# Delta inverse in tiles of 32 and 64, a small projection in four strips, an earlier first norm and a seventh place for expert weights

## The reference, cut to what matters

```
mod  = silu(cond) @ w_mod + b_mod                    # shift1, scale1, gate1, shift2, scale2, gate2
h    = layer_norm(x) * (1 + scale1) + shift1
proj = h @ w_in                                      # among it beta, alpha, i, f: 32 columns
# gated DeltaNet, per direction, head and chunk of 64 tokens:
strict_l = where(strict, beta * (k k^T) * decay, 0)
sol  = triangular_solve(eye + strict_l, [v * beta | k * beta * exp(G)])
u    = u_v - u_k @ s;  o = q_dec @ s + qk @ u;  s = s * g_end + k_dec^T @ u
x    = layer_norm(alpha * x + gate1 * mix, ln1_g, ln1_b)
h    = layer_norm(x) * (1 + scale2) + shift2
hid  = silu(h @ w_e1[e]) * (h @ w_e3[e])             # 2 experts per token, of 32; D_EXPERT = 256
x    = layer_norm(alpha * x + gate2 * sum(gate * hid @ w_e2[e]), ln2_g, ln2_b)
```

## Time and profile before

| | |
|---|---|
| median of 3 runs | 1314.59 us (1314.35 to 1315.8) |
| profiled execution | 1314.85 us, span 1313.1 us, clock granted 0.983 |
| PE busy | 1220.2 us, 93% (its weight loads 728.8) |
| DVE, ACT, POOL busy | 653.3, 288.8, 127.0 us |
| DMA | 221.97 MB, mean 169 GB/s; HBM read 211.52 MB, written 17.78 MB |

### The profile page before, as it was taken

How to read it: one execution, slowest core, us unless ns; L and a number is a source line. 1 busy time by engine, 2 the same in 40 slices (tenths; PEclk the granted TensorE clock), 3 DMA queues, 4 the chain that set the end, 5 groups by cost and what they waited for, 6 DMA issues and landing times. The chain is left out here.

```text
span 1313.1 us, 15161 instructions
## 1 busy us (share of the span) xinstructions
PE 1220.2 (93%) x5699; PEld 728.8 (56%) x5699; DVE 653.3 (50%) x1425; ACT 288.8 (22%) x591; POOL 127.0 (10%) x148
## 2 busy tenths in 40 slices
PE   3899999999999999999999999999999898899775
PEld 1455555556557678566666666665459533344332
DVE  5140366658825435245556675342777434243226
ACT  2200354336134324321111020111001001011002
POOL 0000000000000000000000424420300222122010
PEclk9999999999999999999999999999998999999888
DMA  9533332444022213032110212417519799999936
GB/s 370 233 106 117 129 128 83 174 145 94 28 63 54 78 23 104 1 105 84 56 63 25 96 49 94 179 58 208 212 48 389 267 411 420 420 420 419 411 148 251
DMA packets 64972, 221.97 MB, mean 169 GB/s; under 512 B 21390, under 2 KB 32286, under 8 KB 48254
## 3 DMA queue, kind: packets, MB, share of 16 engines
q1 hardware_dynamic: 59566, 209.39, 42.5%
q0 software_dynamic: 5184, 10.50, 2.1%
q10 hardware_dynamic: 144, 1.05, 0.2%
HBM read 211.52 MB, written 17.78 MB: 175 GB/s over the span
## 5 line engine op out<-in xcount | busy, mean ns | idle before, releaser
L505 PE MATMUL bank<-hT,ring 128*128 128x512 f32 x320 | 165.3, 598 | 0.0
L2943 PE MATMUL bank<-ew,xgT 128*64 128x512 f32 (+2 forms) x544 | 130.8, 622 | 17.9 <-DMA ew<-in_experts 16.1
L506 PEld LDWEIGHTS bank<-hT,ring 128*128 128x128 f32 x320 | 60.8, 190 | 76.5 <-issue 76.5
L2943 PEld LDWEIGHTS bank<-ew,xgT 128*64 128x64 f32 (+2 forms) x544 | 47.5, 144 | 98.3 <-issue 96.0
L981 PE MATMUL bank<-hT,ring 128*128 128x512 f32 x176 | 90.4, 595 | 3.0 <-DVE yA L1487 3.0
L1782 PE MATMUL bank<-hT,w_ab 128*128 128x512 f32 x160 | 81.9, 594 | 0.0
L2957 PE MATMUL bank<-ew,hidT 128*64 128x512 f32 (+2 forms) x272 | 67.4, 629 | 8.2 <-DMA ew<-in_experts 7.1
L2315 PE MATMUL bank<-w_out,mT 128*128 128x512 f32 x160 | 70.9, 604 | 3.2 <-PEq L1655 3.2
L506 PE MATMUL bank<-hT,ring 128*128 128x128 f32 x320 | 61.5, 274 | 0.0
L982 PEld LDWEIGHTS bank<-hT,ring 128*128 128x128 f32 x176 | 33.4, 190 | 42.1 <-issue 42.1
L3079 DVE SCALAR_TENSOR_TENSOR uh<-uh,bank 128x256 f32<-128x256 f32 x18 | 7.6, 421 | 97.8 <-ACT uh L3028 97.8
(11 more groups left out here) (521 smaller groups left out, 2175.7 us busy)
## 6 DMA issues: line engine op xcount, KB each, us to landing
ew<-in_experts SPq DMA_DIRECT2D x96, 1024.0 KB, 27.4
ring<-in_blocks SPq DMA_DIRECT2D x10, 2048.0 KB, 9.5
mhalf<-in_mods SPq DMA_DIRECT2D x16, 1024.0 KB, 5.1
w_p<-in_merge SPq DMA_DIRECT2D x14, 768.0 KB, 5.8
w_ab<-in_merge SPq DMA_DIRECT2D x10, 768.0 KB, 4.4
mstage<-in_mods SPq DMA_DIRECT2D x3, 2048.0 KB, 18.3
w_out<-in_w_out SPq DMA_DIRECT2D x1, 4096.0 KB, 15.0
rows<-mod_rows SPq DMA_DIRECT2D x8, 512.0 KB, 7.3
```

What stands on the lines that cost most here:

```text
L505: pe.matmul(lat[:, :], w, hT[:, k, P:T], start=(k == 0), stop=(k == KD - 1))
L506: mm = pe.matmul(ctx[:, 0:P], w, hT[:, k, 0:P], start=(k == 0), stop=(k == KD - 1))
L2943: mm = pe.matmul(bank[2 + n % 2][hs, :], xgT[:, n % 2, k, hs], ew1[w][k // 4][:, 512 * (k % 4):512 * (k % 4) + 512], start=(k == 0), stop= ...
```

## The change

Four parts. The first norm: DVE makes 1/std and a shift (-mean/std) of a tile as soon as the statistics of the next one are done, and ACT normalises tiles 0 to 3; DVE keeps the last. The fourth block of `in_mods` is loaded in two halves. The small projection goes round four strips of 32 output partitions, all 512-token products first and the 128-token ones behind; a matrix of four stacked unit matrices of 32 (`spn`, three DVE additions) sums the strips in a real product in place of the transpose. The delta inverse: f5 and x5 are 16 products of 32 rows by 32 columns by 32, one for each (head, direction, chunk), in place of 8 of 128 x 128 x 64; dT is 8 products of 64x64 with the unit matrix in place of 8 transposes of 128x128, and one ACT copy of 256 columns in place of two of 512; f6 and x6 use 64 rows of weights; the copies of f5 and f6 are 128 and 256 columns, not 512. The experts: a seventh place of first weights lies where x1 was; x1 is written to DRAM (`residual_rows`) a tile at a time in "out", and read back after the last expert load.

```
-            for m in MODS:
+            for m in MODS[:3]:
                 sp.dma_start(mod_at[m], A["mods"][m]).then_inc(got_mod[m], 16)
+            for f in range(2):
+                sp.dma_start(mod_at[3][:, 2048 * f:2048 * f + 2048], A["mods"][3][:, 2048 * f:2048 * f + 2048]).then_inc(
+                    got_last if f else got_mod[3], 16)
...
+                if t:
+                    act.wait_ge(vs.sem, vs.after("shift", t - 1))
+                    act.activation(x_sb[:, t - 1, :], x_sb[:, t - 1, :], ACT.Identity, scale=rstd[:, t - 1:t],
+                                   bias=shift[:, t - 1:t]).then_inc(as_.step("xn", t - 1), 1)
...
-            for t in range(NT):
-                dve.wait_ge(as_.sem, as_.after("sqrt", t))
-                dve.reciprocal(rstd[:, t:t + 1], rstd[:, t:t + 1]).then_inc(vs.step("rec", t), 1)
-                dve.wait_ge(vs.sem, vs.after("rec", t))
-                dve.tensor_scalar(x_sb[:, t, :], x_sb[:, t, :], mv[:, t, 0:1], rstd[:, t:t + 1], ALU.subtract,
-                                  ALU.mult).then_inc(vs.step("xn", t), 1)
+                if t:
+                    dve.wait_ge(as_.sem, as_.after("sqrt", t - 1))
+                    dve.reciprocal(rstd[:, t - 1:t], rstd[:, t - 1:t]).then_inc(vs.step("rec", t - 1), 1)
+                    dve.wait_ge(vs.sem, vs.after("rec", t - 1))
+                    dve.scalar_tensor_tensor(shift[:, t - 1:t], mv[:, t - 1, 0:1], -1.0, rstd[:, t - 1:t], ALU.mult,
+                                             ALU.mult).then_inc(vs.step("shift", t - 1), 1)
...
             pe.wait_ge(vs.sem, vs.after("xn", NT - 1))
+            pe.wait_ge(as_.sem, as_.after("xn", NT - 2))
...
-            for k in range(KD):
-                pe.matmul(bank[6][0:32, :], w_small[:, k, :], hT[:, k, P:T], start=(k == 0), stop=(k == KD - 1))
-                mm = pe.matmul(bank[7][0:32, 0:P], w_small[:, k, :], hT[:, k, 0:P], start=(k == 0), stop=(k == KD - 1))
+            for out, cs in ((bank[6][:, :], slice(P, T)), (bank[7][:, 0:P], slice(0, P))):
+                for k in range(KD):
+                    lo = 32 * (k % 4)
+                    mm = pe.matmul(out[lo:lo + 32, :], w_small[:, k, :], hT[:, k, cs], start=(k < 4), stop=(k >= 4))
...
+                        pe.wait_ge(v1.sem, v1.after("fold", 2))
                         for t in range(NT):
-                            mm = pe.transpose(bank[6][:, 32 * t:32 * t + 32], tr[0:32, tok(t)], ident[0:32, 0:32])
+                            mm = pe.matmul(bank[6][:, 32 * t:32 * t + 32], tr[:, tok(t)], spn[:, 0:32], start=True, stop=True)
...
+            for i in range(2):
+                dve.tensor_tensor(spn[:, 32 * i:32 * i + 32], ident[:, 64 * i:64 * i + 32], ident[:, 64 * i + 32:64 * i + 64],
+                                  ALU.add).then_inc(v1.step("fold", i), 1)
+            dve.wait_ge(v1.sem, v1.after("fold", 1))
+            dve.tensor_tensor(spn[:, 0:32], spn[:, 0:32], spn[:, 32:64], ALU.add).then_inc(v1.step("fold", 2), 1)
...
+    STRIPS = [(d, c) for c in range(2) for d in range(2)]
+    strip_of = lambda d, c: slice(64 * c + BS * d, 64 * c + BS * d + BS)
+    half_of = lambda d: slice(64 * d, 64 * d + 64)
+    inside = lambda h, s: slice(P * h + s.start, P * h + s.stop)
...
-                for d in range(2):
-                    for h in range(H):
-                        cols = dt_[g % 2][d][:, P * h:P * h + P].rearrange("p (b c) -> p b c", c=BS)[:, 1 - d::2, :]
-                        mm = pe.matmul(bx[:, 256 * d + 64 * h:256 * d + 64 * h + 64], n_all[:, tile_of(g, d), d, h, :], cols, start=True, stop=True)
+                for h in range(H):
+                    for d, c in STRIPS:
+                        to, of = strip_of(d, c), strip_of(1 - d, c)
+                        mm = pe.matmul(bx[to, BS * h:BS * h + BS], n_all[of, tile_of(g, d), d, h, to], dt_[g % 2][d][of, inside(h, of)],
+                                       start=True, stop=True)
                 mm.then_inc(p3.step("f5", g), 1)
 
             def inner_product(g):
                 pe.wait_ge(a3.sem, a3.after("f5", g))
                 if g:
                     pe.wait_ge(v3.sem, v3.after("qkm", g - 1, 1))
-                for d in range(2):
-                    for h in range(H):
-                        mm = pe.matmul(by[:, 256 * d + 64 * h:256 * d + 64 * h + 64], hd(dd_[d], h), f_[:, d, h, :], start=True, stop=True)
+                for h in range(H):
+                    for d, c in STRIPS:
+                        to = strip_of(d, c)
+                        mm = pe.matmul(by[to, BS * h:BS * h + BS], dd_[d][to, inside(h, to)], f_in[to, BS * h:BS * h + BS],
+                                       start=True, stop=True)
                 mm.then_inc(p3.step("x5", g), 1)
 
             def turned(g):
                 pe.wait_ge(v3.sem, v3.after("x5", g))
-                for d in range(2):
-                    for h in range(H):
-                        mm = pe.transpose(hd((bx, by)[d], h), hd(dt_[g % 2][d], h), ident)
-                    mm.then_inc(p3.step("dT", g, d), 1)
-
-            def outer(g):
-                pe.wait_ge(a3.sem, a3.after("dT", g, 0))
                 for h in range(H):
                     for d in range(2):
-                        half, c = slice(64 * d, 64 * d + 64), P * h + 64 * (1 - d)
-                        mm = pe.matmul(bx[half, 256 * d + 64 * h:256 * d + 64 * h + 64], n_all[:, tile_of(g, d), d, h, half],
-                                       dt_[g % 2][d][:, c:c + 64], start=True, stop=True)
+                        half = half_of(d)
+                        mm = pe.matmul(bx[half, 64 * h:64 * h + 64], dt_[g % 2][d][half, inside(h, half)], ident[half, half],
+                                       start=True, stop=True)
+                mm.then_inc(p3.step("dT", g), 1)
+
+            def outer(g):
+                pe.wait_ge(a3.sem, a3.after("dT", g))
+                for h in range(H):
+                    for d in range(2):
+                        to, of = half_of(d), half_of(1 - d)
+                        mm = pe.matmul(bx[to, 64 * h:64 * h + 64], n_all[of, tile_of(g, d), d, h, to], dt_[g % 2][d][of, inside(h, of)],
+                                       start=True, stop=True)
                 mm.then_inc(p3.step("f6", g), 1)
...
                     for d in range(2):
-                        half, c = slice(64 * d, 64 * d + 64), P * h + 64 * d
-                        mm = pe.matmul(by[half, 256 * d + 64 * h:256 * d + 64 * h + 64], dT_(g, d)[:, c:c + 64], f_[:, d, h, :],
-                                       start=True, stop=True)
+                        half = half_of(d)
+                        mm = pe.matmul(by[half, 64 * h:64 * h + 64], dT_(g)[half, h, :], f_[half, h, :], start=True, stop=True)
                 mm.then_inc(p3.step("x6", g), 1)
...
                 act.wait_ge(p3.sem, p3.after(x, g))
-                act.activation(f_[:].rearrange("p d h c -> p (d h c)"), bx[:, :], ACT.Copy).then_inc(a3.step(x, g), 1)
+                if x == "f5":
+                    act.activation(f_in, bx[:, 0:H * BS], ACT.Copy).then_inc(a3.step(x, g), 1)
+                else:
+                    act.activation(f_[:].rearrange("p h c -> p (h c)"), bx[:, 0:H * 64], ACT.Copy).then_inc(a3.step(x, g), 1)
 
             def turned(g):
-                for d in range(2):
-                    act.wait_ge(p3.sem, p3.after("dT", g, d))
-                    act.activation(dT_(g, d)[:], (bx, by)[d][:, :], ACT.Copy).then_inc(a3.step("dT", g, d), 1)
+                act.wait_ge(p3.sem, p3.after("dT", g))
+                act.activation(dT_(g)[:].rearrange("p h c -> p (h c)"), bx[:, 0:H * 64], ACT.Copy).then_inc(a3.step("dT", g), 1)
...
-        (mT1_off + 24576, mT1_off + 32768), (rows_off + 8192, rows_off + 16384), (rows_off + 24576, rows_off + 32768)))]
+        (mT1_off + 24576, mT1_off + 32768), (rows_off + 8192, rows_off + 16384), (rows_off + 24576, rows_off + 32768),
+        (yA_off, yA_off + 8192)))]
...
+    slot1 = lambda x: x % 7 if x < NE else (x - NE + 4) % 6
+    in_slot = lambda x: [y for y in range(x + 1) if slot1(y) == slot1(x)]
...
                 sp.dma_start(h2d[t * P:t * P + P, :], h2[:, t % 3, :]).then_inc(sent8[t % 3], 16)
+                sp.dma_start(x1d[t * P:t * P + P, :], x1[:, t, :]).then_inc(x1_sent, 16)
...
     def sync_units(sp):
         def first_half(expert, x, i):
-            sp.wait_ge(pt_m.sem[("f1a", "f1")[i]], user_of(x - 6) + 1)
-            load_half(sp, EXPERT(expert), x % 6, i)
+            if x == 6:
+                sp.wait_ge(x1_sent, 16 * NT)
+            else:
+                sp.wait_ge(pt_m.sem[("f1a", "f1")[i]], user_of(in_slot(x)[-2]) + 1)
+            load_half(sp, EXPERT(expert), x, i)
...
-        for i in range(2):
-            for x in (NSTAT, NSTAT + 1):
-                first_half(expert_of(x), x, i)
+        assert NSTAT == 6
+        for x in (NSTAT, NSTAT + 1):
+            first_halves(expert_of(x), x)
...
         rest(NP)
```

(30 more changed lines are left out.)

53 lines of the change are left out of this document (33 added, 20 removed).

## The result

The changed kernel takes 1299.53 us (median of 4 runs, 1298.06 to 1300.74) against 1315.19 (4 runs of before): ratio 0.988, interval 0.986 to 0.990. 1299.3 was forecast. The profiled execution has a span of 1297.3 us, 15.8 less than before.

| place | start before | lead of the changed kernel |
|---|---|---|
| first block product (L505, now L528) | 53.96 | 6.05 |
| behind the fold of the small projection | 63.23 | 5.44 |
| end of the delta stage (L1183) | 525.85 | 17.06 |
| merge, ahead of the normalisation of `h_f` (L1892) | 741.33 | 17.16 |
| merge, behind it (L1892) | 779.09 | 12.08 |

The account below looks back on a forecast made before the run. TensorE was taken to bound the kernel up to 1029 us, then the expert-weight loads. Terms 0 - 5.6 - 7.2 - 2.7 = -15.5 took 1314.85 to 1299.3 us (chance 58%), range 1292.5 to 1307.5.

Parts of the forecast that it names:

- the two regimes: Whole kernel: TensorE bounds from 60 to 1029 us, the loads of expert weights from 1040 to 1245 us.
- First norm: First norm and modulation block: earlier normalised rows gain nothing, as TensorE's modulation product ends equally late; 0, bounds -0.3 and +0.5.
- Small projection: Small projection before the first block product: 10.2 us become 3.9, the fold costs 0.6 more; net -5.6 us.
- Rival E: Start of the kernel: the gain ahead of 60 us is lost to a load that doesn't move; 1304.9 us, chance 3%.
- Delta inverse: Delta stage: ten f5 and x5 steps fall from 1.73 to 1.1 us each, the turn saves 0.9; -7.2 us.
- rival D: Delta inverse: small products run at array time, 0.6 us a step, DVE holding back some; 1294.3 us, chance 12%.
- rival A: Delta inverse: the strips don't overlap, a step stays at 1.73 us and gains nothing; 1305.6 us, chance 9%.
- C: Delta inverse: small products keep 0.108 us a record, a step takes 3.46 us; slower, 1322.9 us, chance 4%.
- nearly all is gained: Delta stage: the f5 and x5 savings pass through, since DVE still isn't last, by 0.3 us.
- The seventh place: Ahead of the expert units: the seventh expert's weights load at once and fill a DMA hole, residual copy free; -2.7 us.
- Rival B: Tail takes back the seventh place, by second-weight places or slow DMA engines (1302.0) or residual reads in series (1305.5); chance 13%.
- seven signs: Trace checks listed beforehand, among them f5 at 1.1 us, units reached 12 to 13 us earlier, last expert 2 to 3 sooner.

Follow-up runs that it names:

- e5: Changed kernel with the two loops of f5 and x5 swapped, so four heads of one strip run one after the other: 1303.68 us, ratio 0.9896.
- e3: Kernel before with only the seventh place of first weights and the residual through memory: 1313.43 us, ratio 0.9981.
- e6: Changed kernel without the writes of x1 to DRAM and the reads back, a result row added in place of the residual: 1300.27 us, ratio 0.987.
- e7: Changed kernel with 160 no-operations on TensorE in the first large projection, which left no instruction in the trace: 1297.71 us, ratio 0.9846.
- e9: Kernel before with 128 more waits, on semaphores long reached, on TensorE in chunks 0 to 15 of the first large projection: 1319.04 us, ratio 1.001.
- e10: Changed kernel with 180 more waits, on semaphores long reached, on TensorE in the first large projection: 1298.19 us, ratio 0.985.
- e2: Kernel before with only the delta inverse's small tiles: 1308.22 us, ratio 0.9932.

## Why the prediction was right, term by term

The total was met by luck: two large terms were off in opposite directions (see the sum). What was right is the picture of the two regimes and the first two terms.

**First norm: right.** 0 forecast, 0.15 lost, with the landing of L171's weights as the common limit.

**Small projection: right.** 3.9 us forecast, 3.99 measured; fold 0.6 and 0.61; the net lead is 5.44 (with the 0.15 above), 5.6 forecast. Rival E is out: 5.34 of it are still there when the delta stage starts.

**Delta inverse: the size was off.** -7.2 forecast with bounds of -11.5 and -3.0, and -11.6 measured, just outside. The step that failed is the price of a 32x32 record: the nearest row (L1091, 0.039 us) was taken as near the truth, and 0.012 was measured. The prediction's own aside, "if only array time counted it would be near 0.4", is what came (0.39 a step), but neither the forecast nor rival D (0.6) used it. f5 and x5 together gained 13.6 us; part of it was held back because DVE became last, as the text had it for f5 under 0.8 us. The overhead that the Trainium skill gives a matmul (TensorEngine Tiling (Array Packing), Instruction Overhead: about 60 cycles) would make a step 0.8 us, an estimate. That is what e5 shows with four products in a row on one strip (0.80), and twice what the alternating order needs (0.39). The prediction called this rule one against the small tiles, but its 0.8 lay below the 1.1 that was forecast. The same page of the Trainium skill, Gotcha 1: PSUM Pressure, says that different row tiles can't use one PSUM bank at once. That would have been rival A; f5 and x5 write one bank from four row tiles at 0.012 us a record, so it did not bind here. Rivals A and C are out.

**A loss that no rival named.** Behind the delta stage the prediction let the gain pass through, with TensorE idle 22 us in 969 as the argument. The step that failed is "nearly all is gained": DVE and POOL were looked at in the delta stage only. 5.1 us went in the merge, by a chain in which the delta code moved a fetch, the fetch a landing, the landing POOL's sums, these DVE's normalisations, and the wait TensorE's clock. Rival E spoke of a load that doesn't move; here one came 1.4 us too soon. The Trainium skill has the link between the two engines (GPSIMD Engine Reference, Key points: GpSimd shares its SBUF interfaces with VectorE, and they contend when DVE runs in a mode with two ports or reads two SBUF inputs). The traces agree that they contend: the normalisation, one tensor in SBUF, takes 1.8 us instead of 0.34 beside a sum, while a DVE sum with one input in PSUM kept its 0.49 us. Which of the two conditions the normalisation meets no run shows.

**The seventh place: about right.** -2.7 forecast. From the order's arrival (lead 12.62) to the end (15.8) 3.2 us were gained, 3.4 in e3, about 3 between the averages of the profiles. "Up to 1031 nothing can be done" was read too late: the order is known at 1028.64, and before the change the DMA engines are 0.88 and 0.60 busy in the two us from 1029 to 1031, so half a us more could be filled. The first sorted load goes out 4.8 us earlier relative to the start of the units. On the other side TensorE's filler ran at the lower clock level (7.06 us, 5.56 before) and SP entered the units 1.0 us later behind DVE's list than before. Rival B is out by e6, by the reads' 24 us and by the 3 us that reach the end.

**Sum.** -5.4 - 11.6 - 0.1 + 5.5 (from 17.16 to 11.70, merge and its end) - 0.9 (up to the order) - 3.2 = -15.7, the profile's 15.8 but for rounding. The forecast -15.5 met it because 4.4 us more than forecast in the delta stage and a loss of 5.5 in the merge nearly cancel. The -0.9 is nobody's term: it lies within the spread of that stretch from profile to profile. Of the seven signs listed, three failed: f5's pace; TensorE's lead at the units, 11.6 where 12 to 13 were expected; and the landing of the last expert relative to the first unit, 3.6 us sooner where 2 to 3 were expected (1265.69 and 1029.51 before, 1250.49 and 1017.87 after).

## What to carry to other kernels

A total that comes out right proves no term: compare start times of the same instruction through both traces, stage by stage. In small tiles let consecutive products change strips; here that halved their time again (0.80 to 0.39 us a step). Where DVE normalises SBUF data, keep POOL's elementwise work out of the way with a wait that costs little (0.5 us here), since otherwise a landing that moves by a microsecond, if only because code has grown elsewhere, can decide over several.

## What the runs showed of the hardware that was not expected

A 32x32x32 product in f32 takes 0.012 us a record with four strips in turn and 0.025 on one strip. One DVE normalisation of 128x128 takes 0.34 us alone and 1.8 to 1.97 beside POOL. With a fetch of 16 KB of instructions inside it, a load of 1.5 MB landed its last piece after 7.4 to 7.8 us, without one after 6.2 to 6.7. Waits of 2.8 to 3.7 us on TensorE were followed by the lower clock level in six profiles (after, e5, e6, e7, e9, e10) and not in a seventh (e2).
